# A diagonal of reciprocals in place of the identity in the turning product of an attention stage

## The reference, cut to what matters

```python
# layer 0 of the second block (8 heads of 64)
#   latent queries: 256 latent keys (with a bias) and 256 context keys
#   context queries: 256 context keys
# layer 1 of the second block, latent queries only
#   8 heads with a window, 256 latent and 256 context keys, and a sink
#   4 differential heads: softmax(one) - lam * softmax(other)
s = q @ k.T * 64 ** -0.5 + bias
p = exp(s - max(s)) / sum(exp(s - max(s)))      # sum includes exp(sink - max) where there is a sink
o = p @ v
```

## Time and profile before

| | us |
|---|---|
| median of three runs | 2596.15 |
| lowest and highest of them | 2588.34, 2597.18 |
| the profiled execution's own time | 2593.33 |
| its span in the trace | 2591.4 |
| PE busy | 2521.1 (97%) |
| DVE busy | 1525.6 (59%) |
| ACT busy | 601.5 (23%) |
| POOL busy | 757.5 (29%) |

### The profile page before, as it was taken

One profiled execution on the slowest core, in us unless ns is written; L12 is line 12 of the kernel. 1 busy time (PEld: TensorE's weight loads), 2 busy tenths in 40 slices (PEclk: granted clock), 3 DMA queues, 4 the chain that ended last, 5 costly groups with the idle time before them and its releaser, 6 DMA issues.

```text
span 2591.4 us, 40667 instructions
## 1 busy us (share of the span) xinstructions
PE 2521.1 (97%) x16418; PEld 2010.7 (78%) x16418; DVE 1525.6 (59%) x2763; ACT 601.5 (23%) x1293; POOL 757.5 (29%) x580
## 2 busy tenths in 40 slices
PE   8999999999999999999999989999999999999999
PEld 4789888888867777789988868888888776555554
DVE  2897688468858888634664873765555556310112
ACT  1316221100044545422022052100000325201110
POOL 0550045455402112048854400453454120000000
PEclk9999999999999999999999999999999999999999
DMA  9532356465423433644534231555533310599996
GB/s 326 173 119 98 121 196 215 167 237 170 126 74 99 122 81 102 208 147 163 163 126 126 82 130 69 194 185 171 172 132 110 109 34 1 238 416 412 416 404 279
DMA packets 222714, 447.89 MB, mean 173 GB/s; under 512 B 18905, under 2 KB 124184, under 8 KB 219450
## 3 DMA queue, kind: packets, MB, share of 16 engines
q1 hardware_dynamic: 181184, 330.83, 35.6%
q10 hardware_dynamic: 41338, 114.40, 13.6%
HBM read 444.06 MB, written 1.13 MB: 172 GB/s over the span
## 4 chain that ended last, share of the span: by engine, by line
PE 89%; DVE 5%; DMA 2%; ACT 1%; issue 1%; SPq 1%; POOL 1%; ACTq 0%; DVEq 0%; POOLq 0%
PE bank L1393 52%; PE bank L1102 13%; PE bank L3548 5%; PE bank L3567 2%; PE bank_pair L3548 2%; PE bank L1118 1%; PE bank_pair L3567 1%; PE bank L566 1%; DMA slot<-in_ssd_w_in 1%; PE bank L2510 1%; DMA slot<-in_moe_w 1%; PE bank L2503 1%; PE bank L3584 1%; PE bank L3495 1%; PE bank L2735 1%
## 5 line engine op out<-in xcount | busy, mean ns | idle before, releaser
L1406 POOL TENSOR_TENSOR slot<-slot 128x512 f32<-128x512 f32 (+3 forms) x288 | 367.2, 1275 | 1353.3 <-PE bank L1393 899.2
L1393 PE MATMUL bank<-arena,slot 128*128 128x256 f32 (+1 forms) x3704 | 676.4, 343 | 2.6 <-POOL slot L1407 1.2
L1393 PEld LDWEIGHTS bank<-arena,slot 128*128 128x128 f32 x3704 | 604.9, 191 | 66.4 <-issue 3.8
L1393 PE MATMUL bank<-uT,slot 128*128 128x256 f32 (+1 forms) x2472 | 502.6, 360 | 6.3 <-DMA slot<-in_ssd_w_in 3.6
L1393 PEld LDWEIGHTS bank<-uT,slot 128*128 128x128 f32 x2472 | 432.6, 192 | 67.6 <-issue 11.0
L1407 POOL TENSOR_TENSOR slot<-slot 128x512 f32<-128x512 f32 (+3 forms) x288 | 404.7, 1405 | 0.0
L1393 PE MATMUL bank<-slot 128*128 128x256 f32 x848 | 192.1, 379 | 0.0
L1102 PE MATMUL bank<-arena,slot 128*128 128x256 f32 x832 | 182.7, 382 | 1.1 <-DVEq L3858 1.1
L1393 PEld LDWEIGHTS bank<-slot 128*128 128x128 f32 x848 | 160.7, 190 | 26.8 <-issue 5.1
L1102 PEld LDWEIGHTS bank<-arena,slot 128*128 128x128 f32 x832 | 159.5, 192 | 23.4 <-issue 1.6
L1102 PE MATMUL bank<-uT,slot 128*128 128x256 f32 (+2 forms) x576 | 163.6, 438 | 0.0
(11 more groups left out here) (507 smaller groups left out, 3187.5 us busy)
## 6 DMA issues: line engine op xcount, KB each, us to landing
slot<-in_ffn_w SPq DMA_DIRECT2D x42, 2048.0 KB, 9.4
arena<-in_ada_wt ACTq DMA_DIRECT2D x89, 512.0 KB, 3.7
slot<-in_moe_w SPq DMA_DIRECT2D x62, 704.0 KB, 16.7
arena<-in_moe_w SPq DMA_DIRECT2D x52, 704.0 KB, 17.5
rstd<-in_ada_wt ACTq DMA_DIRECT2D x51, 512.0 KB, 3.6
slot<-in_moe_w SPq DMA_DIRECT2D x11, 2048.0 KB, 18.8
uT<-in_ada_wt ACTq DMA_DIRECT2D x32, 512.0 KB, 3.6
slot<-in_ssd_w_in SPq DMA_DIRECT2D x32, 512.0 KB, 8.8
```

What stands on the lines that cost most here:

```text
L1393: ins = pe.matmul(bank[:, u * n:u * n + n], left[:, k, u * P:u * P + P], right[:, k, :], start=(k == 0), stop=(k == self.h - 1))
L1406: pool.tensor_tensor(out[:, :, 0:c], x[:, :, 0:c], y[:, :, 0:c], op)
```

## The change

For units that are not differential, DVE no longer multiplies the 128x`nk` scores by the reciprocals. It multiplies the 128x128 identity by them, row by row, into a tile of its own, so that it holds diag(rc). PE then makes, for each 128x128 piece x of the scores, the ordinary f32 product x.T @ diag(rc) in place of the transpose x.T @ ident. Six such tiles lie at 15872 in the arena (three units deep, two for each). Both forms give the divided and turned probabilities. Signals, order and the number of instructions on each engine stay as they are. Differential units are as before.

```diff
+        m_divide = arena_at(15872, 6, P)
...
                 for t in range(self.units[u]["nk"] // P):
-                    ins = pe.transpose(bank[:, t * P:t * P + P], self.score(u, a)[:, t * P:t * P + P], ident)
+                    out, x = bank[:, t * P:t * P + P], self.score(u, a)[:, t * P:t * P + P]
+                    if self.units[u]["sub"]:
+                        ins = pe.transpose(out, x, ident)
+                    else:
+                        ins = pe.matmul(out, x, self.divisor(u, a), start=True, stop=True)
                 ins.then_inc(B.full_sem, 1)
+
+            def divisor(self, u, a):
+                return m_divide[:, 2 * (u % 3) + a, :]
...
                 dve_link(ch, dve.reciprocal(rc, den))
                 for a in range(2):
-                    s = self.score(u, a)
-                    dve.tensor_scalar(s, s, rc[:, a:a + 1], None, ALU.mult).then_inc(*S("pn").given())
+                    dve.tensor_scalar(self.divisor(u, a), ident, rc[:, a:a + 1], None, ALU.mult).then_inc(*S("pn").given())
```

## The result

The changed kernel takes 2612.13 us (median of five runs, 2607.37 to 2614.96), against 2596.15 before: a ratio of 1.0062, 95% interval 1.0049 to 1.0074. It is slower by 16 us, and the prediction of 2594.1, with a range up to 2599, was wrong. What happened was the third rival, to which the prediction had given 0.04.

What follows compares the result with a forecast made beforehand. In the attention stages no engine was full, with PE, DVE and ACT close and the chain deciding. Gains of 1.2 (even) and 1.1 (odd) less 0.3 for handovers made 2.0 us, from 2596.15 to 2594.1, range 2586 to 2599.

Steps and rivals of the forecast that it cites:

- the third rival: L2958's ordinary product is slower than a transpose: with +0.090 us each, up to 2610.5 us; chance 0.04.
- the price of the product: PE's 160 f32 products in both attention stages: 0.124 us each by L2970, against 0.128 for a transpose.
- The overlap: Even stage: most DVE savings fall where PE holds the chain without a gap; 1.2 us reach the chain.
- the waits: Attention stages: diagonal tiles and ACT's overwriting of scores bring no new wait; ACT's 3.07 us lies under PE's 3.12.
- the next bound: Odd stage: PE is late next, with turn, outputs and scores end to end at 3.12 us a unit.
- its own sign of being wrong: In the changed kernel's timeline, a product at L2958's successor of 0.14 us or more would show the forecast wrong.
- The upper bound: A 256-column product takes 0.218 us, 0.090 more than a transpose; on all 160 that makes +14.4 us.
- The rival's formula: Slow product at L2958: a loss from 0.013 us more a product, measurable as slower from (13 + 2) / 160 = 0.094.
- DVE's term: L3067's pair of multiplications takes 0.40 us at 128 columns, against 0.80 at 512 and 0.53 at 256.
- The charge for handovers: Six chain handovers from DVE to PE pay 0.05 us each for longer weight loads: 0.3 us.
- The gain by DVE alone: Cheaper DVE multiplications shorten the even stage by 1.2 us and the odd one by 1.1.
- Row against rule: PE's product: trace rows within 4 ns of a transpose, against the skill's factor of four, 0.51 us a product.

Runs made afterwards that it cites:

- the odd half alone: The change in the odd stage only, the even stage dividing in place and transposing as in the kernel before: 2601.07 us, 1.0027 to the kernel before.
- the bf16 kernel: The changed kernel with scores and diagonals of the non-differential units stored as bf16, product summed into f32: 2588.98 us, 0.9981 to the kernel before.

## Why the prediction was wrong

- **The step that failed** is the price of the product: "The nearest row of a product with the same shape [...] is L2970: eight take 2159.81 - 2158.82 = 0.99 us, 0.124 us each." The eight rows of that turn are four products. The kernel's text says so: `outputs` makes one product for each of the four key blocks of a differential unit, eight units make 32, and the trace of before has 64 instructions on that line:

```profile
L2970 PE MATMUL bank<-arena,uT x48: 275/275/347, 2158.8 to 2177.5; 128*128 128x128 f32 x48
L2970 PE MATMUL bank_pair<-arena,uT x16: 275/275/275, 2161.6 to 2168.0; 128*128 128x128 f32 x16
```

  Transposes on L2958 are 192 for 192 in the source. The same pairs could be seen in the earlier trace rows: the two products of `scores` stand there as x4, the eight of `outputs` as x16. The count would have given 0.248 us a product, 0.12 more than a transpose, and on a PE that the prediction itself had found full in the odd stage, 3.12 + 8 x 0.12 = 4.1 us a unit. Measured: 4.06. The overlap, the waits and the next bound of the prediction held; its own sign of being wrong, a product of 0.14 us or more, is what came.
- **The upper bound was low by the same slip.** 0.218 us for 256 columns is also one of two instructions, and I used it to bound a whole product. The rival's formula, with 0.094 us more a product as the threshold of a measurable loss, was right: the real surcharge is 0.12, and PE is busy for 11.0 + 8.3 = 19.3 us more, of which 16.3 reached the stages' ends. The rest went into gaps that PE had had: outside its busy time it has 3.0 us less in the two stages. Of the 16.3 some 1.2 are the clock at the start of the odd stage, as the odd half alone shows, which grew by 6.45 and not 7.55 for the same 64 products.
- **DVE's term was right.** A pair of diagonals takes 0.40 us to its follower (0.48 for the two with the overlap, 0.284 for one) as worked out from two widths. L3095's 0.35 us was no guide. The changed kernel, even stage:

```profile
1519.12 0.48 DVE L3074 TENSOR_SCALAR arena<-const,small 128x128 f32<-128x128 f32 x2
1519.52 0.28 DVE L3098 COPY arena<-bank_pair 128x128 f32<-128x128 f32 x1
```

- **PE as the next bound was right.** 3.12 us a unit was forecast and 3.11 measured once the product was taken out.
- **The charge for handovers** (0.3 us for weight loads of 192 ns against 140) is not seen. The loads are 192 ns as forecast, but from the start of a diagonal to the first instruction of the turn there are 0.34 us with products (1519.12 to 1519.46) and 0.34 with transposes in the kernel that doesn't use the diagonals (1519.62 to 1519.96), and a turn behind a wait is 0.07 us longer than one in a stream in both forms: 2.05 against 1.98 with products, and 1.09 against 1.02 with the transposes of the kernel before.
- **The gain by DVE alone** was forecast at 2.3 us before the charge for handovers and was 1.75. The odd stage gave 1.2 for 1.1. The even one gave 0.5 for 1.2: a cycle took 10.92 us and not 10.74. The two turns of eight pieces in the cycle are some 0.05 and 0.12 us longer on the chain than before; why was not tried.
- **Row against rule.** The rule that I set against the row, that a transpose is four times as fast for FP32 ("TensorE: Matmul & The Clock Gate" in the Trainium skill, section Terms), errs in size, not in sign: 1.98 to 1.02 us for eight, 1.9 times. The advice in "Perfetto Trace Analysis" in the Trainium skill, section Transposes, to use a transpose for one, is borne out for f32. And "FP8 and Floating Point Precision" in the Trainium skill, section TensorE Precision Notes, says that true FP32 takes four passes through the array; the trace shows two instructions for an f32 product and one for a bf16 one and for a transpose, and how many passes are inside each no run here shows.

## What to carry to other kernels

Before a row is taken as the price of an operation, divide the number of its rows by the number of operations that the source issues; here 64 rows for 32 products held the whole answer. The count alone is no price either: a PE instruction followed the one before it by 0.124 us in an f32 product of 128x128 by 128x128, 0.11 in a stream of f32 transposes, 0.069 in the bf16 product and 0.064 in the products of L2973 with 64 columns of weights. In this kernel folding a cheap DVE multiplication into a transpose lost in f32, at two instructions a product, and gained in bf16, at one shorter one. No run has an f32 product of one instruction, so the two reasons are not told apart. And when two engines lie within 10% of each other in a stage, work moved from one to the other has to be priced on the receiver first.

## What the runs showed of the hardware

On DVE the next instruction starts half a pair's time behind the start of a multiplication by a column of scalars, f32 from SBUF to SBUF: 0.40 us at 512 columns, 0.265 at 256 and 0.20 at 128 (the two lines beside DVE's term above). At a quarter of the width half of the cost is still there.

The lower granted clock at the first turn of the odd stage made it nearly twice as long: it took 3.71 us there against 1.98, behind 3.47 us in which PE had nothing to do.

```profile
2135.05 3.78 PE L2963 MATMUL bank_pair<-arena,uT 128*128 128x128 f32 x16 [3.47 <-DVE arena L3074]
2138.76 2.08 PE L2952 MATMUL bank<-arena 64*128 64x512 f32 x4
```

Granted there is 1.2 GHz:

```profile
2135.00:2138.50 3.50, 3.45 (x16) 3.45 (x16) 2.79 (x12) 1.77 (x6) 0.00 (x0) 0.50 0.01 0
```

The granted clock of the 7.00 us from the start of that turn is not the same in all kernels. The changed kernel, the kernel before and the odd half alone:

```profile
2135.05:2142.05 7.00, 7.00 (x31) 5.27 (x32) 3.88 (x16) 4.10 (x14) 0.00 (x0) 0.59 0.00 0
2129.01:2136.01 7.00, 7.00 (x42) 4.24 (x43) 6.34 (x24) 5.98 (x19) 0.00 (x0) 0.76 0.00 0
2128.95:2135.95 7.00, 7.00 (x44) 5.90 (x46) 4.87 (x21) 4.90 (x15) 0.00 (x0) 0.76 0.01 3
```

The first turn of the kernel before lost 0.85 us (1.87 against 1.02), that of the changed kernel 1.73. This is not a price of the products: the odd half has the same products and lost no more over the 7.00 us than the kernel before, and the bf16 kernel, with its single instructions, was granted 0.58 there. What counts is how much of the stretch runs at 1.2 GHz, and the difference of 0.17 is 1.2 of the odd stage's 7.6 us. What sets it no run here shows.
